# Attention by head pairs with the values stationary in halves, and the zeros for scratch written later

## The reference

```python
qg = q.reshape(B, rows, GRID_W, H, Dh)
kg = k.reshape(B, rows, GRID_W, H, Dh)[:, row_idx]
vg = v.reshape(B, rows, GRID_W, H, Dh)[:, row_idx]
s_loc = jnp.einsum('brchd,brjkhd->bhrcjk', qg, kg) * scale + bias
s_loc = jnp.where(col_mask[:, None, :], s_loc, -jnp.inf)
s_ctx = jnp.einsum('brchd,bmhd->bhrcm', qg, k_ctx) * scale
s = jnp.concatenate([s_loc.reshape(B, H, rows, GRID_W, n_loc), s_ctx], axis=-1)
p = jax.nn.softmax(s, axis=-1)
out = einsum('bhrcjk,brjkhd->brchd', p_loc, vg) + einsum('bhrcm,bmhd->brchd', p_ctx, v_ctx)
```

## Time and profile before

| | |
|---|---|
| time, median of 3 runs (lowest to highest) | 751.68 us (749.96 to 753.31) |
| the profiled execution: its own time | 752.79 us |
| the profiled execution: span of the trace | 750.9 us |
| mean granted clock of TensorE, as a share of full speed | 0.964 |
| busy: TensorE, its weight loads | 673.5 us (90%), 412.1 us (55%) |
| busy: VectorE, ScalarE, GpSimd | 226.1, 159.3, 151.2 us |
| chain that ended last: TensorE, DMA, VectorE, SP's queue | 83%, 6%, 5%, 2% |

### The profile page before, as it was taken

One profiled execution on the slowest core, in us unless ns is written; L12 is line 12 of the kernel. 1 busy time (PEld: TensorE's weight loads), 2 busy tenths in 40 slices (PEclk: granted clock), 3 DMA queues, 4 the chain that ended last, 5 costly groups with the idle time before them and its releaser, 6 DMA issues.

```text
span 750.9 us, 11852 instructions
## 1 busy us (share of the span) xinstructions
PE 673.5 (90%) x4923; PEld 412.1 (55%) x4923; DVE 226.1 (30%) x505; ACT 159.3 (21%) x330; POOL 151.2 (20%) x186
## 2 busy tenths in 40 slices
PE   0899999997999999999989999999999999999600
PEld 0656556564458888544477546566546654654400
DVE  0510099900034554232377101111101011110157
ACT  4202210201146675211221011010111001111042
POOL 5107840900033450031111100000100000000040
PEclk9999999998999999999998999999999999999955
DMA  9986860994039430074172899979999999994184
GB/s 249 385 271 128 242 225 1 347 332 175 1 122 390 190 115 2 0 292 184 65 301 70 282 358 326 383 275 400 380 390 392 417 360 412 407 410 176 45 288 131
DMA packets 50663, 186.17 MB, mean 248 GB/s; under 512 B 7152, under 2 KB 9577, under 8 KB 46384
## 3 DMA queue, kind: packets, MB, share of 16 engines
q1 hardware_dynamic: 43408, 163.18, 59.0%
q0 software_dynamic: 7088, 22.17, 9.0%
q10 hardware_dynamic: 112, 0.04, 0.0%
HBM read 163.13 MB, written 22.31 MB: 247 GB/s over the span
## 4 chain that ended last, share of the span: by engine, by line
PE 83%; DMA 6%; DVE 5%; SPq 2%; ACT 1%; issue 1%; POOL 1%; POOLq 0%; DVEq 0%; ACTq 0%
PE bank L1728 11%; PE bank L1735 10%; PE bank L1584 9%; PE bank L1465 7%; PE bank L1751 6%; PE bank L1760 5%; PE bank L1525 5%; PE bank L1412 4%; PE bank L1626 4%; DMA slots<-in_w_ada 3%; PE bank L1428 3%; PE bank L1743 3%; PE bank L1470 2%; PE bank L1715 2%; SPq L444 2%; DMA x<-in_x_prompt 2%
## 5 line engine op out<-in xcount | busy, mean ns | idle before, releaser
L1465 PE MATMUL bank<-ra,slots 128*128 128x512 f32 x192 | 83.3, 594 | 0.4 <-DVE ra L843 0.4
L1584 PE MATMUL bank<-slots,rc 128*128 128x512 f32 x160 | 69.9, 593 | 0.0
L1465 PEld LDWEIGHTS bank<-ra,slots 128*128 128x128 f32 x192 | 36.1, 190 | 45.6 <-issue 44.6
L1154 DVE TENSOR_TENSOR rc<-re,bank 128x256 f32<-128x256 f32 (+1 forms) x32 | 10.2, 359 | 160.8 <-PE bank L1735 88.5
L1353 POOL COPY gi<-ridx 128x1 uint32<-128x1 uint32 x18 | 3.6, 198 | 272.8 <-PE bank L1715 237.7
L1728 PE MATMUL bank<-rb,rc 128*128 128x512 f32 x128 | 56.2, 595 | 0.0
L858 DVE SCALAR_TENSOR_TENSOR re<-re,cwT 128x670 f32<-128x670 f32 x60 | 52.3, 945 | 0.0
L554 ACT ACTIVATE rb<-bank 128x512 f32<-128x512 f32 (+1 forms) x64 | 31.1, 525 | 94.7 <-PE bank L1465 49.6
L1584 PEld LDWEIGHTS bank<-slots,rc 128*128 128x128 f32 x160 | 29.9, 190 | 34.9 <-issue 34.9
L1735 PE MATMUL bank<-slots,rc 128*64 128x256 f32 x384 | 43.7, 382 | 0.0
L1241 POOL TENSOR_TENSOR mod<-mod,vecT 128x8 f32<-128x8 f32 (+1 forms) x8 | 19.6, 2455 | 117.9 <-ACT mod L554 117.9
(11 more groups left out here) (296 smaller groups left out, 989.2 us busy)
## 6 DMA issues: line engine op xcount, KB each, us to landing
slots<-in_w_ada SPq DMA_DIRECT2D x12, 2048.0 KB, 12.5
slots<-in_moe_w_gate SPq DMA_DIRECT2D x8, 2048.0 KB, 12.7
rb<-in_moe_w_gate SPq DMA_DIRECT2D x8, 2048.0 KB, 11.4
rb<-in_moe_w_up SPq DMA_DIRECT2D x8, 2048.0 KB, 14.5
rb<-in_moe_w_down SPq DMA_DIRECT2D x8, 2048.0 KB, 12.2
slots<-in_moe_w_up SPq DMA_DIRECT2D x8, 2048.0 KB, 14.5
slots<-in_moe_w_down SPq DMA_DIRECT2D x8, 2048.0 KB, 14.1
slots<-in_w_in SPq DMA_DIRECT2D x4, 2048.0 KB, 14.0
```

Source lines behind the costliest of these rows:

```text
L1465: ins = mm(b[:, :], w[:, k, m * P:(m + 1) * P], hT[:, k, 0:NLAT], start=k == 0, stop=k == KD - 1)
L1584: ins = mm(b[:, :], mT[:, k, i * P:(i + 1) * P], wo[k // 4][:, k % 4, 512 * hf:512 * hf + 512], start=k == 0, stop=k == KD - 1)
```

## The change

In TensorE's program a step is now a pair of heads (16 steps, `score` and `values`), and side work takes one piece a step at the step's end. The values are now the stationary side, 64 columns of one head, and the turned probabilities the moving side, 128 columns. The two heads of a pair go into the two column halves of the array and the two halves of the bank's partitions, so the result comes out with channels on the partitions, and no second turn of it is needed. The sums now come from ScalarE's exp (`accum_out`), over all 512 scores in one instruction, which reads PSUM; VectorE writes the masked scores back to PSUM for it. The reciprocals of the sums are spread to 128x512 by VectorE (`spread`), turned by TensorE (`R`, in place of `aT`), copied, and multiplied with the result into `mT` (`weigh`). Banks go by role: scores 0 to 3, turned probabilities 4 and 5, results, `R` and side work 6 and 7. `take` waits for whatever piece had the bank before. ScalarE copies turned probabilities ahead of the next exps (`TAKEN` is its order). The three writes of zeros move from n = 12 to n = 15 of SP's list. GpSimd's fetch of modulation rows (`modr`, `bc`) moves behind its mask loop.

```diff
-            if n == 12:
+            if n == 15:
 
                 sp.wait_ge(S["zeros_ready"], 1)
                 sp.dma_start(t["yd"][NE * P:BIG * P, :].rearrange("(q p) n -> p q n", p=P),
...
         act.wait_ge(S["zeros_out"], 16 * 3)
-        for i in range(STEPS):
-            for u in (i, i + 1) if i < PAIRS and i % 2 == 0 else ():
+        for j in range(STEPS):
+            for s in (2 * j - 2, 2 * j - 1) if 1 <= j < PAIRS + 1 else ():
+                ge(act, "pv_done", j - 1)
+                b = filled(act, "PT", s)
+                evac(pts[:, s % 2, :], b[:, :])
+            for u in (2 * j, 2 * j + 1) if j < PAIRS else ():
                 act.wait_ge(S["smax_done"], u + 1)
                 b = filled(act, "S", u)
-                nmx = st[:, 2, u:u + 1]
-                sc.activation(pr[:, u % 4, 0:256], pr[:, u % 4, 0:256], ACT.Exp, bias=nmx)
-                evac(pr[:, u % 4, 256:512], b[:, 256:512], ACT.Exp, bias=nmx)
...
+                evac(pr[:, u % 4, :], b[:, :], ACT.Exp, bias=st[:, 2, u:u + 1], accum_out=st[:, 0, u:u + 1])
...
+        def spread(tile):
+
+            emptied(dve, "S", 8 * tile + 7)
+            one = rw[:, 8 * tile:8 * tile + 8]
+            link(v.reciprocal(one, st[:, 0, 8 * tile:8 * tile + 8]))
...
+            v.tensor_copy(at.rearrange("p (h e) -> p h e", h=H),
+                          one.unsqueeze(2).to_broadcast([P, H, DH])).then_inc(S["spread_ready"], 1)
+
+        def weigh(tile):
+
+            dve.wait_ge(S["pv_done"], 4 * tile + 4)
+            b = filled(dve, "R", tile)
+            evac(at, b[:, :])
+            emptied(dve, "R", tile)
+            v.tensor_tensor(mT[:, 0:4, tile * P:(tile + 1) * P], bank[6 + tile % 2][:, :].rearrange("p (m n) -> p m n", m=4),
+                            at.rearrange("p (m n) -> p m n", m=4), ALU.mult).then_inc(S["mixed_ready"], 1)
...
+        def values(pair):
+
+            tile, m = pair // 4, pair % 4
+            if m == 0 and tile >= 1:
+                emptied(pe, "R", tile - 1)
+            for u in range(2):
+                emptied(pe, "PT", 2 * pair + u)
+            for q in range(4):
+                for u in range(2):
+                    h = 2 * m + u
+                    v = (vl[:, tile, h, 0:DH], vl[:, (tile + 1) % 4, h, 0:DH], vc[:, 0, h, 0:DH], vc[:, 1, h, 0:DH])[q]
+                    ins = mm(bank[6 + tile % 2][64 * u:64 * u + 64, m * P:(m + 1) * P], v, pts[:, u, q * P:(q + 1) * P],
+                             start=q == 0, stop=q == 3)
+            ins.then_inc(S["pv_done"], 1)
...
+        for j in range(STEPS):
+            if j < PAIRS:
+                score(j)
...
+            if 2 <= j < PAIRS + 2:
+                values(j - 2)
+            for s in (2 * j - 2, 2 * j - 1) if 1 <= j < PAIRS + 1 else ():
+                emptied(pe, "S", s)
+                transposes(("PT", s), [pr[:, s % 4, q * P:(q + 1) * P] for q in range(4)])
+            if j < PAIRS:
+                for key in BESIDE.get(j, ()):
+                    ge(pe, "mixed_ready", (j - 3) // 4)
+                    beside[key[0]](*key[1:])
+            if j >= 5 and j % 4 == 1:
+                pe.wait_ge(S["spread_ready"], j // 4)
+                ge(pe, "mixed_ready", j // 4 - 1)
+                transposes(("R", j // 4 - 1), [at[:, m * P:(m + 1) * P] for m in range(4)])
```

More of the change, by code:

```diff
@@ L912, in _ @@
         beside = {"Sc": prompt_scores, "wo": add_mixed}
[L913 to L926, removed]
+        for j in range(STEPS):
+            for u in (2 * j, 2 * j + 1) if j < PAIRS else ():
+                b = filled(dve, "S", u)
+                link(v.tensor_reduce(st[:, 0, u:u + 1], b[:, 256:512], AX.X, ALU.max))
+                dve.wait_ge(S["bm_ready"], u + 1)
+                link(v.tensor_tensor_reduce(b[:, 0:256], b[:, 0:256], bm[:, u % 4, :], 1.0, st[:, 0, u:u + 1],
+                                            ALU.add, ALU.max, st[:, 1, u:u + 1]))
+                v.tensor_scalar(st[:, 2, u:u + 1], st[:, 1, u:u + 1], -1.0, None, ALU.mult).then_inc(S["smax_done"], 1)
+            for key in BESIDE.get(j, ()):
+                if key[0] in beside:
+                    beside[key[0]](*key[1:])
+            if j >= 4 and j % 4 == 0:
+                spread(j // 4 - 1)
+            if j >= 5 and j % 4 == 1:
+                weigh(j // 4 - 1)
         for i in range(TT):
@@ L933, in _ @@
             if i == 0:
-                norm(8)
-                norm(9)
+                norm(0)
+                norm(1)
             dve.wait_ge(S["ssq2_ready"], i + 1)
@@ L1308, in _ @@
         pool.wait_ge(S["raw_in"], 16 * 16)
-        for s in range(PAIRS):
+        for s in range(2 * PAIRS):
             if s >= 4:
@@ L1391, in take @@
         def take(*key):
[L1393 to L1398, removed]
+            if PRIOR[key] is not None:
+                emptied(pe, *PRIOR[key])
             return bank[BANK[key]]
@@ L1591, in aT, with score @@
         def aT(i):
-            pe.wait_ge(S["o_free"], 2 * i + 2)
+            pe.wait_ge(S["o_free"], 2)
             transposes(("aT", i), [at[:, m * P:(m + 1) * P] for m in range(4)])
[L1595 to L1598, removed]
+        def score(pair):
+            tile, m = pair // 4, pair % 4
+            rows = [slice(64 * u, 64 * u + 64) for u in range(2)]
+            b = [take("S", 2 * pair + u) for u in range(2)]
+            for u, p in enumerate(rows):
+                mm(b[u][:, 0:256], qT[p, m, tile * P:(tile + 1) * P], kT[p, m, tile * P:tile * P + 256],
+                   start=True, stop=True)
+            for u, p in enumerate(rows):
+                give(mm(b[u][:, 256:512], qT[p, m, tile * P:(tile + 1) * P], kcT[p, m, :],
+                        start=True, stop=True))
@@ L1637, in _ @@
             emptied(pe, "PTc", j)
-            ob = o_bank(8 + j)
+            if j == 0:
+                emptied(pe, "R", 3)
+            else:
+                pe.wait_ge(S["mixed_ready"], 4)
+            ob = bank[6 + j]
             for q in range(4):
```

136 lines of the change are left out of this document (53 added, 83 removed).

## The result

The changed kernel takes 764.22 us in the median (763.73 to 765.55, 4 runs) beside 752.15 us (749.96 to 753.31, 4 runs) for the kernel before on the same chip: a ratio of 1.0167 with a 95% interval of 1.0139 to 1.0194. The forecast was 765.0 (756 to 772). The profiled execution took 763.73 us with a span of 761.8 us, so 1.9 us lie outside it, as before.

The account below looks back on a forecast made before the run. TensorE was taken to bound the attention. 6.6 us gained, the wait for zeros and a 64.75 us stretch put the output projection 13.6 us later: 752.79 + 13.6 = 766.4, less 1.1: 765 us (756 to 772).

Parts of the forecast that it names:

- `ada` 7, 6.6 us earlier: Ahead of the attention: TensorE's 4.84 us idle before `ada` 7 and 1.76 us of low clock go, 6.6 us earlier.
- The zeros land at 245.4: SP's queue: zeros behind the load of `ada` 9, issued at 210.55, land 34.85 us later, at about 245.4.
- ScalarE waits, TensorE waits behind it: Attention's entrance: ScalarE's first exp waits for the zeros, TensorE stalls about 25 us, transposes begin at 246.2.
- Values at 1.08 a pair: Attention, TensorE: 0.88 us for a pair's values plus 0.2 for changes of shape; the values save 9.6 us.
- Cold start, 2.0: After some 25 us of idle time TensorE restarts at the lower clock level, costing 2.0 us.
- The tail, 1.0: End of the attention: TensorE waits about 1.0 us for the last two exps.
- The rest does what it did: Attention: transposes `R` cost what `aT` cost; other side work and the prompt's scores cost what they did.
- The sum: First transposes to output projection: 64.75 us from 246.2, so it starts at 311.0 against 297.37, 13.6 us later.
- The rest follows unchanged: Behind the start of the output projection at about 311, everything takes what it took before.
- 1: Attention: ScalarE bounds a pair (3.4 us, time 769), or the array's halves do not overlap (779); chance 0.09.
- 2: Zeros land sooner, at 239.9, but not soon enough; time 760, or 757 with no price for shapes; chance 0.11.
- 3: No stall if zeros land before 231.8: stretch 62.75 us, output projection at 282.2, time 736; chance 0.08.

Follow-up runs that it names:

- zeros_only: The kernel before, with only the three writes of zeros moved from n = 12 to n = 15; 773.92 us, ratio 1.0299.
- behind_ada7: The changed kernel with the writes of zeros issued right behind the load of `ada` 7, ahead of the wait for `ada` 8's slot; 735.34 us, ratio 0.9786.
- values_twice: behind_ada7 with the 16 instructions of each pair's values made twice into the same bank; 748.33 us in one run.
- warm_gap2: The changed kernel with 120 idle matmuls (240 instructions) in TensorE's gap ahead of the first transposes of probabilities; 764.24 us, ratio 1.0164.
- late_zeros: The changed kernel with zeros written from a tile the attention doesn't use, issued behind all 19 loads; 734.51 us, ratio 0.9773.
- other_banks: behind_ada7 with scores in banks 4, 5, 0 and 1 and transposes in 2 and 3; 734.78 us, ratio 0.9777.
- own_tile: The changed kernel, zeros still at n = 15 but from a tile the attention doesn't use, ScalarE's wait for them moved behind the attention; 746.16 us, ratio 0.9917.

## Why the prediction was right, and which terms were off

The mechanism, its place and its sign were as predicted. Term by term:

- *`ada` 7, 6.6 us earlier.* Right: the load of `ada` 9 goes out at 210.47 (210.55 predicted), where it was 217.15.
- *The zeros land at 245.4.* They landed at 246.9, 1.5 us late. The prediction took the DMA engines as otherwise empty; in fact GpSimd writes 512 KB of new keys and values beside the sequence, which that of before did not share. The mean rate is the same, and 0.57 MB more at 345 GB/s are 1.6 us. No run moved these writes away.
- *ScalarE waits, TensorE waits behind it.* Right, and shown by `zeros_only` and `behind_ada7`. Transposes begin 0.83 us behind the start of the exp (0.8 predicted).
- *Values at 1.08 a pair.* 1.02, since the fixed share is 0.14 us and not 0.2 (`values_twice`); the values save 26.99 - 16.43 = 10.6 us, not 9.6. A pair is 3.10, not 3.17.
- *Cold start, 2.0.* Mis-sized: 0.97 on the path (`warm_gap2`). The price was taken from `ada` 7, which waits for nothing inside; here 0.7 of the 1.7 us of slower work covered a wait for an exp.
- *The tail, 1.0.* 0.73 us.
- *"The rest does what it did".* Not quite: the fourth `R` stands ahead of the output projection, where its `aT` stood behind the first piece (0.59 us more in the stretch), and the first eight transposes wait for the second exp (1.33 us in `behind_ada7`, 1.02 elsewhere). On the other side the transposes of `ada`'s rows took 0.33 us instead of 0.92 and the prompt's scores 1.64 instead of 2.17; these pieces stand in other neighbourhoods now. Without the cold start the stretch is 61.3 us, not 62.75.
- *The sum.* 62.28 instead of 64.75 us, and a landing 1.5 us later: the output projection starts at 310.02 (311.0 predicted), 12.65 us later than before. Two errors of opposite sign met, so that this start is only 1 us off is partly luck.
- *"The rest follows unchanged".* Off by 1.8 us: the first expert tile starts 10.8 us later (412.22 against 401.43 before). Of this 0.5 is the fourth `R`, which is no longer behind the first piece of the output projection. From the third piece on to the table of slots it is 77.5 us in both, so the hidden edits cost nothing. The other 1.4 us lie in the table's last piece (2.38 instead of 2.78 us) and the 36 idle instructions: these took 6.96 us at a low clock before (0.58, in the row below this list), and here 4.26 us, 5.97 with the wait for the gathered rows. The span grew by 10.9 us: 752.79 + 10.9 = 763.7, the profiled execution's own time. So the two traces differ by 10.9 us where 13.6 were forecast, and the medians by 12.1; that the median of 764.22 lies 0.8 from the forecast is partly luck too.
- *Not foreseen:* 0.83 us of waiting for the fixed banks, ahead of the gap and so free in the changed kernel.

The kernel before, its 36 idle instructions (the columns are those of the earlier trace rows):

```profile
394.40:401.40 7.00, 7.00 (x39) 7.00 (x39) 5.93 (x27) 0.00 (x0) 3.06 (x4) 0.58 0.40 103
```

Of the rivals, 1 is refuted by the 1.02 us and by TensorE's 15.60 of 15.60 us in `behind_ada7`; 2 by the landing; 3 was right on its price and wrong on its condition. The three fastest versions differ from the changed kernel by where the zeros stand (`late_zeros` also by their tile, `other_banks` by its banks): 735.3 (`behind_ada7`), 734.5 (`late_zeros`) and 734.8 us (`other_banks`), not to be told from one another.

## What to carry to other kernels

A transfer moved along an in-order queue is priced at both places: what it held where it was, and everything that stands behind it, or shares its tile, where it goes. Removing one of two waits may only uncover the other (`own_tile`): look for a place where nothing is behind. Idle work that keeps a clock up belongs where it ends ahead of the real wait even at the low clock, or it becomes the wait.

## What the runs showed of the hardware

- Two writes that span 32 and 64 partitions moved at about 210 GB/s together, against some 420 for the one over 128 partitions, at both places in the program.
- On TensorE 16 instructions for the values behind scores of another shape took 1.02 us and 32 took 1.90: 0.14 us come as a fixed price, which the change of shape would explain.
- At the lower clock, a restart after 27 us of waiting cost 1.7 us of slower work (granted clock 0.53), of which only 0.97 reached the end of the stretch.
- Of a gain of 1.8 us ahead of a stretch of idle matmuls (`warm_gap2`) 0.6 were left behind it: the granted clock was 0.61 there, against 1.00 in the changed kernel, and 36 instructions took 6.64 us instead of 4.26.
